# Another order of loads and stores in SyncE's queue, in the middle stage of a decoder layer's step

## The reference

```
h = modulate(rms_norm(x, g_pre_mix), shift_m, scale_m)
u, q, k, v, z_pool, z_att = split(h @ w_in)
y_pool = pool_mix(u_ext, ...) @ w_proj_pool              # moving means over 2, 4, 8, 16 tokens, one map per group
# samples: for each of 3 head groups (window, dilation) = (128,1), (512,4), (2048,16)
s = einsum('btsd,btjsd->btsj', q, kg) * HEAD_DIM**-0.5    # kg: cached keys gathered by stride, and the new key
p = exp(s - max(s)); o = einsum('btsj,btjsd->btsd', p, vg) / sum(p)
y_att = merge_groups(outs, lses) @ w_proj_att
mix = (sigmoid(z_pool) * y_pool + sigmoid(z_att) * y_att) @ w_out
x = x + gate_m * rms_norm(mix, g_post_mix)
# then the feed-forward part: w_up, a causal convolution of width 3, GeGLU, w_down
```

## Time and profile before

| | us |
|---|---|
| median of 3 runs (1113.83 to 1115.45) | 1115.17 |
| the profiled execution | 1115.0 |
| its span | 1113.1 |

### The profile page before, as it was taken

One profiled execution on the slowest core, in us unless ns is written; L12 is line 12 of the kernel. 1 busy time (PEld: TensorE's weight loads), 2 busy tenths in 40 slices (PEclk: granted clock), 3 DMA queues, 4 the chain that ended last, 5 costly groups with the idle time before them and its releaser, 6 DMA issues.

```text
span 1113.1 us, 20437 instructions
## 1 busy us (share of the span) xinstructions
PE 1029.6 (92%) x8597; PEld 976.7 (88%) x8597; DVE 481.2 (43%) x879; ACT 399.0 (36%) x636; POOL 119.4 (11%) x165
## 2 busy tenths in 40 slices
PE   5999999999999999998678893799999999999996
PEld 3899999999999999988657892799999999999994
DVE  5533324332432234246544336655556655422224
ACT  5434323432343234321113223654445455322223
POOL 1000300040004000604414004000000000000000
PEclk8899999999999999999889895799999999999996
DMA  9976677666756675245964645166666666555402
GB/s 328 257 269 209 201 228 250 196 205 229 255 187 217 221 260 185 88 162 193 394 230 160 206 158 194 36 222 224 224 219 221 227 222 203 163 164 160 120 25 77
DMA packets 227720, 222.30 MB, mean 200 GB/s; under 512 B 6269, under 2 KB 191997, under 8 KB 226845
## 3 DMA queue, kind: packets, MB, share of 16 engines
q1 hardware_dynamic: 227629, 220.99, 60.6%
HBM read 213.56 MB, written 96.03 MB: 278 GB/s over the span
## 4 chain that ended last, share of the span: by engine, by line
PE 84%; DMA 4%; DVE 4%; POOL 3%; ACT 2%; SPq 2%; issue 1%; ACTq 0%; POOLq 0%; DVEq 0%
PE acc L1295 72%; DMA qB<-sample_qkv 3%; PE psS L1459 2%; PE psT L1473 2%; PE psS L1339 2%; PE acc L1553 1%; POOL tha L665 1%; POOL cached L659 1%; POOL ssq L625 1%; DMA ada_first<-in_w_ada 1%; PE psS L1447 1%; PE psT L1487 1%; SPq L341 1%; PE psS L1349 1%; PE psS L1445 1%
## 5 line engine op out<-in xcount | busy, mean ns | idle before, releaser
L1295 PE MATMUL acc<-act_hi,w_hi 128*128 128x260 f32 x1920 | 399.9, 290 | 24.3 <-DVE w_lo L905 9.5
L1295 PE MATMUL acc<-act_hi,w_lo 128*128 128x260 f32 x1920 | 390.8, 286 | 0.0
L1295 PE MATMUL acc<-act_lo,w_hi 128*128 128x260 f32 x1920 | 390.3, 285 | 0.0
L905 DVE TENSOR_TENSOR w_lo<-raw,w_hi 128x1024 fp32r<-128x1024 f32 (+1 forms) x148 | 186.5, 1261 | 393.0 <-ACT w_hi L686 392.4
L1295 PEld LDWEIGHTS acc<-act_hi,w_hi 128*128 128x128 f32 x1920 | 300.7, 192 | 34.0 <-issue 17.2
L1295 PEld LDWEIGHTS acc<-act_lo,w_hi 128*128 128x128 f32 x1920 | 300.6, 191 | 0.0
L1295 PEld LDWEIGHTS acc<-act_hi,w_lo 128*128 128x128 f32 x1920 | 300.3, 191 | 0.0
L686 ACT ACTIVATE w_hi<-raw 128x1024 fp32r<-128x1024 f32 (+1 forms) x148 | 154.8, 1046 | 212.4 <-PE acc L1295 163.5
L1295 PE MATMUL acc<-g_hi,w_hi 128*128 128x260 f32 x352 | 71.1, 283 | 0.0
L1295 PE MATMUL acc<-g_hi,w_lo 128*128 128x260 f32 x352 | 70.8, 282 | 0.0
L1295 PE MATMUL acc<-g_lo,w_hi 128*128 128x260 f32 x352 | 70.6, 282 | 0.0
(11 more groups left out here) (237 smaller groups left out, 948.9 us busy)
## 6 DMA issues: line engine op xcount, KB each, us to landing
out_k_sample<-in_cache_k_w SPq DMA_DIRECT2D x89, 368.0 KB
out_v_sample<-in_cache_v_w SPq DMA_DIRECT2D x89, 368.0 KB
raw<-in_w_in SPq DMA_DIRECT2D x60, 512.0 KB, 5.7
raw<-in_w_up SPq DMA_DIRECT2D x44, 512.0 KB, 5.7
ada_mid<-in_w_ada SPq DMA_DIRECT2D x11, 1024.0 KB, 9.4
ada_first<-in_w_ada SPq DMA_DIRECT2D x9, 1024.0 KB, 10.7
raw<-in_w_down SPq DMA_DIRECT2D x16, 512.0 KB, 3.9
out_k_sample<-in_cache_k_w SPq DMA_DIRECT2D x16, 511.0 KB
```

Of the source, the lines that this page charges most:

```text
L905: dve.tensor_tensor(w_lo[PLACE[n]][:, 0:cols], raw[:, n % RAW, 0:cols], w_hi[PLACE[n]][:, 0:cols].bitcast(F32), ALU.subtract).then_inc(lo_ ...
L1295: ins_ = pe.matmul(acc[b][:, half, 0:HALF], w, x[:, t, half * HALF:(half + 1) * HALF], start=first and i == 0 and j == 0, stop=last and i ...
```

## The change

The same loads and stores are issued, with the same waits on their slots. Between the issue of key 1 and that of value 4 the order on SyncE is another: tile 2 and keys 2 and 3 stand ahead of the wait for the sample rows; the wait for their store and the first two query loads follow it at once, then tile 3, and only then the six small stores; value 0 stands ahead of query 2 and key 4; the rows for the softmax (with their wait for `o_lod`) go from ahead of key 2 to behind value 1; query 5 goes ahead of value 2 and tile 7. VectorE gets one wait more, for `o_lod`, ahead of reduction 0.

```diff
             load_k(1)
+            proj_pool(2)
+            load_k(2)
+            load_k(3)
 
             sp.wait_ge(smp_ready, 1)
             sp.dma_start(scratch.rearrange("m b n -> (m b) n"), smp_rows[0:3 * NG * NB, :]).then_inc(smp_stored, 16)
+            sp.wait_ge(smp_stored, 16)
+            load_q(0)
+            load_q(1)
+            proj_pool(3)
             for g in range(NG):
                 for kv in range(2):
                     o = outs["new"][g][kv][1][0, :, WINS[g] - 1].rearrange("b s d -> b (s d)")
                     r0 = ((1 + kv) * NG + g) * NB
                     sp.dma_start(o, smp_rows[r0:r0 + NB, :]).then_inc(new_rows, 16)
-            sp.wait_ge(smp_stored, 16)
-            load_q(0)
-            load_q(1)
-            proj_pool(2)
-            sp.wait_ge(o_lod, PAIRS)
-            sp.dma_start(bh[0:NB * NS, :, :], scratch.rearrange("m b (h d) -> (b h) m d", d=HD)).then_inc(smp_back, 16)
-            load_k(2)
-            load_k(3)
-            proj_pool(3)
             proj_pool(4)
+            load_v(0)
             load_q(2)
             load_k(4)
-            load_v(0)
             proj_pool(5)
             load_q(3)
             load_k(5)
             load_v(1)
+            sp.wait_ge(o_lod, PAIRS)
+            sp.dma_start(bh[0:NB * NS, :, :], scratch.rearrange("m b (h d) -> (b h) m d", d=HD)).then_inc(smp_back, 16)
             proj_pool(6)
             load_q(4)
+            load_q(5)
             load_v(2)
             proj_pool(7)
-            load_q(5)
             load_v(3)
             proj_att(0)
             load_v(4)
...
                 dve.wait_ge(prod_done, i + 1)
+                if i == 0:
+                    dve.wait_ge(o_lod, PAIRS)
```

## The result

The changed kernel takes 1107.48 us, the median of 5 runs (1104.79 to 1109.76), against 1115.17 for 5 runs of the kernel before (1111.09 to 1116.48): ratio 0.9933, 95% interval 0.9906 to 0.9961. It is faster by 7.5 us, more than the 0.2% that can be told from no change. The profiled execution took 1109.76 us, with a span of 1108.0 and a mean granted clock of 0.957, against 1115.0, 1113.1 and 0.957 before. So the profile shows 5.1 us of span gained and the medians 7.7: the execution that was profiled is the slowest of the five.

A forecast was written before the change was run, and what follows sets the result against it. Key 4's issue, then the saturated queue and work behind it, was taken to bound the stage. Key 4 3.9 us earlier plus 1.3 us gave 5.2: 1115.0 to 1109.8, median 0.2 higher, 1110.0 us; range 1103 to 1113.5.

The forecast's parts named there:

- rival A: Tile 3's split precedes product 2, or L1066 precedes product 0; key 4 at 517, gain 9.4 us, 1105.8 us; chance 0.36.
- What bounds the kernel: Stage before the score transposes: its end follows key 4's issue, the queue's remaining loads and the work behind them.
- Part 1: Tile 2, keys 2 and 3 fill an idle DMA window; the store behind them ends at 497.2, queries about 3 us later.
- Part 2: Six small stores moved behind tile 3 on SyncE, 1.9 us; tile 3 lands near 506, so TensorE's 5.29 us gap goes.
- Part 3: VectorE operations on two SBUF tiles wait for running GpSimd products; key 4 issued at 521.2, 3.9 us earlier.
- query 2's landing: Query 2 issued when product 0 ends, landing at 513.2: 502.1 plus 4 units, 11.1 us.
- border of 513.8: When VectorE is ready for tile 3's split; product 2 starting later lets that split run first.
- The forecast's case: Product 2 goes before tile 3's split, reduction 0 ends at 521.2; 1108 to 1112 us, chance 0.48.
- Part 4: Key 4 to the transposes at L1561 takes 35.3 us, before 36.6, gaining 1.3 us; transposes at 556.5.
- B: Queue only shifted: product 0 catches L1064 too, key 4 at 522 to 523, distance 36.6; 1112.5 us; chance 0.11.
- C: Slower: query 5's wait for product 3 empties the queue, tile 7 lands beyond 554.8; 1118.2 us; chance 0.05.
- D: Queries no earlier, tile 3's saving eaten by tile 2's blocked w_lo, reduction 0 unmoved; chance counted inside B's 0.11.

The follow-up runs named there:

- The repeat: The changed kernel run and profiled once more with no edit: 1105.06 us, ratio 0.9922.
- the first profile: The profiled execution of the unedited changed kernel in its first session: 1109.76 us, span 1108.0 us.
- part 1 alone: Kernel before with only tile 2 and keys 2 and 3 moved ahead of the wait for the sample rows: 1108.99 us, ratio 0.995.
- value-0: Changed kernel with value 0 put back behind key 4 in SyncE's queue: 1110.92 us, ratio 0.9979.
- query-5: Changed kernel with query 5 put back behind tile 7, as in the kernel before: 1104.12 us, ratio 0.9915.
- the run with the values late: Changed kernel with reductions one unit earlier, plus tile 7 and query 5 ahead of values 1 to 3, reduction 5 ahead of tile 7's split: 1099.48 us.
- the kernel with the store first: Changed kernel with keys 2 and 3 behind queries 0 and 1, so the store stands only behind tile 2: 1107.08 us, ratio 0.9945.
- The run with the reductions first: Changed kernel with score reductions 0 to 4 on VectorE each ahead of the split they stood behind: 1103.93 us, ratio 0.9914.

## Why the prediction was right, and where it was off

The forecast was 1110.0 us with a range from 1103.0 to 1113.5. The median is 1107.48: inside the range, between the band of the forecast (1108 to 1112, chance 0.48) and that of rival A (1103 to 1107, chance 0.36), and nearer to rival A's 1105.8. The repeat's median, 1105.06, is rival A's. For the profiled execution the sum said 1109.8 and it took 1109.76. That agreement is luck, as the steps show.

*What bounds the kernel.* Right. The chain still ran through key 4, and in all the kernels run the transposes followed key 4's issue by 34.6 to 40.9 us, with key 4 anywhere between +10.8 and +25.9. The longest distance is that of the kernel before with early reductions, where key 4 is issued into a full queue. The length behind the transposes was 551.5 us against 551.4 in the first profile, and 549.5 in the repeat.

*Part 1, the store behind the keys.* Right, against the change's favour: expected 5.6 us of waiting (491.59 to 497.2), measured 5.7 and 6.1, and 2.0 with the keys moved away. The Trainium skill's rule in "DMA: Bandwidth & Descriptors", on queues, rings and completion order, agrees with these numbers; a store that passed would have taken the 2.7 us of before. Product 0 started 4.98 and 4.69 us after the queries' issue; 4.9 was reckoned. Counted from the store's issue, at 489.71 here and 491.59 before, it came at 10.7 against the 10.5 of the prediction, so the start at 500.40 instead of 502.1 is the earlier start of the whole stage.

*Part 2.* Right as far as it was tried. Tile 3 was in time in both profiles, and no wait behind the small stores shows. The gap before tile 3 went with part 1 alone too, and the place of the small stores was not run by itself.

*Part 3, which engine has the operands.* The mechanism was right: a split took 5.01 or 5.00 us when it met a product near its start and 1.21 when not, and the value-0 and query-5 runs turn one into the other by moving a load alone. The Trainium skill's lock rule in "SBUF — State Buffer", section "Who interferes with whom", agrees. The sequence, though, never came as a whole. In the first profile only its last link did: product 0 caught L1064 and product 1 caught L1066 (3.81 and 4.33 us, where L1064 was to be free and product 0 to catch L1066), tile 2's split was free and not blocked, and tile 3's was blocked. In the repeat every link but the last came. Key 4 went out at 520.50 in the first profile, 0.7 us before the 521.2 of the sum: product 0 began 1.7 us early, query 2 took 0.65 us longer, and product 2 lasted 5.05 us and not 4.6.

*The term that was mis-sized* is query 2's landing: 4 units of 2.78 us behind the start of product 0, 11.1 us. It was 11.75 us in the first profile (512.15 − 500.40) and 12.8 in the repeat (515.12 − 502.33), and between 11.75 and 12.9 in all eight profiles of kernels with this queue up to query 2. With the usual 12.4 the prediction's own sum is 502.1 + 12.4 = 514.5, behind its border of 513.8, and that is rival A: key 4 at 516.99 in the repeat, where 517 was written. (The transposes are then at 553.31, 1.0 behind the 552.3 that goes with it.) The prediction put the border 0.6 us away and gave the rival 0.36; with this term rightly sized rival A was the likelier case. The forecast's case came in the first profile because the slow pool-map unit held up the join and the splits and not the queries, which no step of the prediction had.

*Part 4, what follows key 4.* Nearly right: 35.3 us expected, 36.0 and 36.3 measured, so 0.3 to 0.6 us of the promised 1.3 came. In the first profile query 3 landed at +9.8 behind key 4 (10.2 expected), query 4 at +21.4 (20.3), tile 7 at +27.8 (27.2): over the loads between the two queries a unit took 3.2 us (2.9 in the repeat) rather than 2.78. That tile 7's split meets product 5 was expected and seen (2.59 us), and the query-5 run shows what it costs. The softmax's rows, the last value and the wait on o_lod cost nothing that shows, as reckoned. TensorE waited 4.55 us for tile 6, where about 4 was said, and 10.82 before the transposes, where 11 was said.

*What was not in the sum.* The clock. The stage began 2.3 us earlier than in the profile before (the first pool-map unit at 477.15 and not 479.49); the granted clock before 100 us was 0.97 and not 0.93. From there to pool tile 0's unit the slow stretch cost 3.3 us (23.1 and not 19.8). So that unit started 1.0 us late; key 4 came 1.7 us earlier behind it than reckoned (+20.2 and not +21.9), and the distance was 0.7 longer. The three cancel, which is why the profiled time came out to within 0.1 us. The two profiles of the changed kernel are 5.2 us apart in span.

*The rivals.* B fell: key 4 came at 520.50 or earlier, not at 522 to 523. Its premise did come true in the first profile, where product 0 caught L1064. C fell: tile 7 landed at 548.3, against 548.4 reckoned and a border of 554.8. D fell: tile 3's gap is gone, and part 1 alone is worth 5.5 us although the queries do come later.

## What to carry to other kernels

Where one reduction or one freed slot decides when a saturated queue may be fed, look for what stands ahead of it in program order on its own engine: here moving the reductions by one unit gave 6 us more, nearly as much as the whole reordering of the queue, and on the old order of the queue the same edit gave only 1.9. A load that lands earlier is not always better: a query that arrived 3 to 4 us sooner started a product on GpSimd just before a subtraction on VectorE and cost 2.5 to 3.5 us at the next key load. Where two such operations stand within 1 us of each other in a timeline, write down both orders as two outcomes, weigh them by how well the terms between them are known, and look at a second profile before explaining a difference of 2 or 3 us.

## What the runs showed of the hardware

- The granted clock fell to 0.50 (1.2 GHz) in the pool-map unit of one execution, after 1.51 us of idleness, and stayed at 1.00 in another of the same kernel, after 1.67 us, and in the kernel before, after 1.51 us. It cost 2.5 us (9.83 against 7.33), and no row of either execution shows a reason. It came once more, in part, in the run with the values late (8.25 us, clock 0.57).
- A queue that is full does not always move the same: 338, 276 and 305 GB/s in the kernel with the store first, and 391, 374 and 354 in the repeat, in the same stretch and with the DMA engines as busy. There the way from key 4 to the transposes was 3.3 us longer. The run with the reductions first had it too (352, 332 and 294 GB/s in its three windows from 6 us behind key 4 on, against 400, 403 and 325 in the repeat), and it stays unexplained.
- A VectorE operation that waits for GpSimd comes in between two products that follow at once, and the second then pays: two products back to back took 10.04 us with L1064 caught between them, and 9.02 in the pair at 541.93 of the same execution, which met none in between. Three of them took 15.48 us in the value-0 run.
